# Three small reorderings in a decoder trunk: a split spread, conv taps inside the fourth slab, and two steps of the opening taken earlier

## The reference, cut to what matters

```
e = silu(c @ cond_w + cond_b)
shift, scale, gate = split(e @ ada_w[i] + ada_b[i])      # 9 vectors of 1024 for a layer
h = rms_norm(x, g) * (1 + scale) + shift
x = x + 0.5 * gate * ((silu(h @ w1) * (h @ w3)) @ w2)     # SwiGLU sublayers
u = glu(h @ w_in + b_in); v = depthwise_conv31(u) + dw_b  # Conformer
x = x + gate * (silu(layer_norm(v)) @ w_out + b_out)
```

## Time and profile before

| what | us |
|---|---|
| median of 3 runs | 1976.34 (1975.79 to 1976.45) |
| the profiled execution's own time | 1978.21 |
| its span in the trace | 1976.4 |
| TensorE matmuls busy | 1945.8 (98%) |
| VectorE busy | 1110.3 (56%) |
| ScalarE busy | 661.9 (33%) |
| GpSimd busy | 150.5 (8%) |
| DMA | 275.88 MB, mean 140 GB/s |

### The profile page before, as it was taken

One profiled execution on the slowest core, in us unless ns is written; L12 is line 12 of the kernel. 1 busy time (PEld: TensorE's weight loads), 2 busy tenths in 40 slices (PEclk: granted clock), 3 DMA queues, 4 the chain that ended last, 5 costly groups with the idle time before them and its releaser, 6 DMA issues.

```text
span 1976.4 us, 24087 instructions
## 1 busy us (share of the span) xinstructions
PE 1945.8 (98%) x9444; PEld 1562.6 (79%) x9444; DVE 1110.3 (56%) x1351; ACT 661.9 (33%) x742; POOL 150.5 (8%) x101
## 2 busy tenths in 40 slices
PE   6999999999989999999999999999999999999999
PEld 5788888876577888888888888888778788888887
DVE  4865564589888565633666533246569774333222
ACT  3422222242254322222432222234248743222211
POOL 0100000121411000001100000111022020000000
PEclk9999999999989999999999999999999999999999
DMA  9454544436413545432354522323245323222232
GB/s 394 170 206 176 206 165 166 158 106 180 126 55 138 208 174 194 175 124 93 116 213 170 191 93 79 102 100 124 95 99 137 107 86 107 85 106 85 88 98 90
DMA packets 50777, 275.88 MB, mean 140 GB/s; under 512 B 7456, under 2 KB 8096, under 8 KB 25760
## 3 DMA queue, kind: packets, MB, share of 16 engines
q1 hardware_dynamic: 47648, 270.87, 39.0%
q10 hardware_dynamic: 3072, 4.23, 0.9%
HBM read 251.94 MB, written 2.10 MB: 129 GB/s over the span
## 4 chain that ended last, share of the span: by engine, by line
PE 89%; DVE 4%; ACT 2%; issue 1%; DMA 0%; ACTq 0%; DVEq 0%; SPq 0%
PE ps L1491 27%; PE ps L1493 26%; PE ps L1492 26%; PE ps L1734 2%; PE ps L1512 1%; PE ps L1837 1%; PE ps L1853 1%; PE ps L1823 1%; PE ps L1619 1%; PE ps L1519 1%; DVE w L896 0%; PE ps L1532 0%; PE ps L1537 0%; PE ps L1531 0%; ACT h_hi L676 0%
## 5 line engine op out<-in xcount | busy, mean ns | idle before, releaser
L1491 PE MATMUL ps<-h_hi,w 128*128 128x512 f32 x1552 | 610.5, 393 | 1.2 <-DVE h_lo L995 1.0
L1493 PE MATMUL ps<-h_hi,w 128*128 128x512 f32 x1552 | 605.0, 390 | 0.0
L1492 PE MATMUL ps<-h_lo,w 128*128 128x512 f32 x1552 | 604.8, 390 | 0.0
L1491 PEld LDWEIGHTS ps<-h_hi,w 128*128 128x128 f32 x1552 | 291.7, 188 | 74.2 <-issue 12.8
L1493 PEld LDWEIGHTS ps<-h_hi,w 128*128 128x128 f32 x1552 | 291.5, 188 | 61.2
L1492 PEld LDWEIGHTS ps<-h_lo,w 128*128 128x128 f32 x1552 | 291.8, 188 | 58.8
L896 DVE TENSOR_TENSOR w<-raw,w 128x1408 fp32r<-128x1408 f32 (+1 forms) x104 | 201.0, 1933 | 204.4 <-ACT w L630 204.4
L630 ACT ACTIVATE w<-raw 128x1408 fp32r<-128x1408 f32 (+1 forms) x104 | 164.7, 1583 | 418.0 <-PE ps L1493 405.8
L1491 PE MATMUL ps<-g_hi,w 128*128 128x512 f32 x704 | 274.5, 390 | 0.0
L1493 PE MATMUL ps<-g_hi,w 128*128 128x512 f32 x704 | 274.2, 389 | 0.0
L1492 PE MATMUL ps<-g_lo,w 128*128 128x512 f32 x704 | 274.2, 389 | 0.0
(11 more groups left out here) (217 smaller groups left out, 1710.8 us busy)
## 6 DMA issues: line engine op xcount, KB each, us to landing
raw<-up_d SPq DMA_DIRECT2D x88, 1024.0 KB, 6.4
ada_raw<-ada_d SPq DMA_DIRECT2D x64, 1024.0 KB, 4.8
raw<-down_d SPq DMA_DIRECT2D x64, 704.0 KB, 4.1
raw<-mix_d SPq DMA_DIRECT2D x28, 1024.0 KB, 4.8
stage<-ada_d SPq DMA_DIRECT2D x12, 1024.0 KB, 20.1
stk<-parted SPq DMA_DIRECT2D x32, 256.0 KB, 4.0
stk<-parted SPq DMA_DIRECT2D x32, 128.0 KB, 2.3
u_blk<-u SPq DMA_DIRECT2D x48, 64.5 KB, 2.0
```

The source lines that it names most:

```text
L1491: pe.matmul(dst, a_hi_, b_hi_, start=start, stop=False, skip_group_check=True)
L1492: pe.matmul(dst, a_hi_, b_lo_, start=False, stop=False, skip_group_check=True)
L1493: return pe.matmul(dst, a_lo_, b_hi_, start=False, stop=stop, skip_group_check=True)
```

## The change

There are three edits.

1. Opening. On ScalarE `hi(N_UP[0] + 1)`, the rounding of slab 1, moves from behind the last chunk's square to the head of chunk 4, behind the wait for the second half of x. On TensorE `start_group(3)` moves from step 3 of the first slab to step 2.
2. `spread` is cut in two parts. For the six norms but the first, the high diagonal's matmul stays ahead of step 5; the low diagonal's and `bias_sums` come 3 matmuls later, between the two output chunks of step 5. (Norm 2 runs both together, as before.)
3. Conv. `conv_taps(0)` no longer stands ahead of `conv_in(3)`, but inside it, ahead of its step 2.

```
@@ ScalarE, opening
             for c in range(4, KD):
                 act.wait_ge(x_in_s[1], 16)
+                if c == 4:
+                    hi(N_UP[0] + 1)
                 entry_high(0, c)
                 square(0, c, x[:, c, :], x_in_s[1], 16)
-            hi(N_UP[0] + 1)
             root(0)
@@ TensorE, first_slab
-                    if k == 3 and m == 0:
+                    if k == 2 and m == 0:
                         start_group(3)
                     if k == 5 and m:
-                        spread(m)
-                        bias_sums(m)
+                        spread_part(m, 0)
                     ...
                     for b in range(2):
                         last = triple(...)
+                        if k == 5 and b == 0 and m:
+                            spread_part(m, 1)
+                            bias_sums(m)
@@ TensorE
+            def spread_part(m, part):
+                pe.wait_ge(rdiag_done, 2 * m + part + 1)
+                last = pe.matmul(row, ones_r[:, :], (fac_hi, fac_lo)[part], start=(part == 0), stop=(part == 1),
+                                 skip_group_check=True)
+                if part:
+                    last.then_inc(row_done, 1)
@@ TensorE, conv_in
+                if c == LAG + 1:
+                    two_chunks(c % 2, pair[c % 2], None, lambda: conv_taps(0), 2).then_inc(slab_done, 1)
+                    return
@@ TensorE, the loop
             for c in range(KD):
                 conv_in(c)
-                if c >= LAG:
+                if c > LAG:
                     conv_taps(c - LAG)
```

More of the change, by code:

```diff
@@ L1606, in sums @@
                 add(sq_tmp[:, 1, :], False, True, stat_done)
+            def spread_part(m, part):
[4 more added lines that the diff above has]
+                    last.then_inc(row_done, 1)
             def spread(m):
[L1610 to L1613, removed]
+                for part in range(2):
+                    spread_part(m, part)
             def ada_reduce(q):
```

## The result

| | before | changed |
|---|---|---|
| median, us | 1976.24 (1975.79 to 1977.04, 6 runs) | 1984.87 (1983.97 to 1985.43, 6 runs) |
| ratio | | 1.0043, 95% interval 1.0033 to 1.0053 |
| profiled execution, its span | 1978.21, 1976.4 | 1985.26, 1983.5 |

Slower by 8.6 us, where I had forecast 6.2 and a range up to 1984.6. The direction was right, the size was too small and the time lies outside the range. Between the two profiled executions there are 7.1 us, and they are to be seen at three places: the opening, the conv's slab 3 and the split spreads.

What follows compares the result with a forecast made beforehand. TensorE, busy 98% of the span, was taken as the bound. Opening + 1.4, spread - 0.5, conv + 3.6 and its clock + 1.7 sum to + 6.2 us: 1976.34 becomes 1982.5 us, eight-in-ten range 1979.8 to 1984.6.

Steps and rivals of the forecast that it cites:

- The conv's wait: Ahead of conv slab 3: TensorE idle 4.3 us in place of 0.8, waiting for VectorE's low half; + 3.6 us.
- The conv's clock: Behind the gap ahead of conv slab 3: granted clock falls to half speed; + 1.7 us.
- The spread: Five norms with a first slab: splitting removes the wait for the low diagonal, partly taken back by GpSimd; - 0.5 us.
- The opening: First slab's steps: ScalarE stands for slab 1's transfer, delaying chunk 4 and TensorE, with a likely clock fall; + 1.4 us.
- I take + 1.4, nearer to the fall: Opening's low spread: chosen between + 0.5 us without a clock fall and + 1.9 us with one.
- the start of step 4 at 39.2: Opening: TensorE starts step 4 at 39.2 in place of 37.51, after a gap of 2.7 us.
- The base: Whole kernel: the + 6.2 us sum from the 1978.21 us profiled execution, applied to the 1976.34 us median, giving 1982.5 us.
- The clock holds: Rival, opening and conv gaps: no clock fall in either, + 3.6 us in all, 1980.0 us; chance 0.07.
- The row that I argued from: Attention stage: TensorE stood 2.06 us, then the clock fell for 3.4 us, losing 1.7 us of matmul time.
- Long slow stretches: Rival, opening and conv gaps: longer half-speed stretches in both, + 8.1 us in all, 1984.4 us; chance 0.10.
- Slab 3's low half does not hold TensorE: Rival, conv: taps inside slab 3 just remove the 0.80 us wait; + 0.1 us in all, 1976.4 us; chance 0.05.
- slab 1 lands early: Rival, opening: slab 1 on the chip by 34.4, not 35.7; with the case before - 3.6 us, 1972.7; chance 0.04.

Runs made afterwards that it cites:

- experiment 7: Only the taps moved inside slab 3, with 18 extra matmuls filling the gap ahead of slab 3's wait, against the kernel before: 1981.05 against 1976.52 us.
- experiments 10 and 11: Against before, conv unchanged: 10 has group 3 ahead of step 2, slab 1 rounded behind chunk 7's high half, 1974.94 us; 11 adds the split spread, 1974.85 us.
- experiment 2: Only the opening's edit (slab 1 rounded ahead of chunk 4, group 3 ahead of step 2) against the kernel before: 1978.85 against 1976.37 us.
- experiment 1: The kernel before, unchanged, profiled once more: median 1976.48 against 1976.37 us, span 1974.8 us.
- experiment 8: Only the taps moved inside slab 3, with slab 3's rounding and low half made earlier, against the kernel before: 1983.73 against 1976.52 us.

## Why the prediction was wrong

**The conv's wait: right.** Slab 3's start, its releaser and the length of the gap came as worked out. Nothing was taken back behind it.

**The conv's clock: right in kind and size.** 1.7 predicted, 1.6 by experiment 7.

**The conv against the median: short by 0.8** (5.3 against 6.1). The 0.8 us wait for `u_blk`, which the edit takes away, I booked as a steady 0.80 of gain. It is there in only some executions, and where it is missing there is less to win. Over the nine profiles with the conv unchanged it is 0.35 on average, so this is worth some 0.45. The rest, about 0.3, I can't place: from norm 1's to norm 3's high spread these nine take 186.7 to 188.9 us, 187.5 on average. The wait for `u_blk` makes part of that spread; most of the rest is the slow stretch behind the conv, 10.2 us in seven of them and 13.6 in experiments 10 and 11, where the way from chunk 1's taps to norm 3 takes 145.1 us in place of 143.6 to 143.9. The changed kernel and edit 3 alone take 193.1 and 193.3.

**The spread: right.** - 0.5 predicted, - 0.6 in the traces.

**The opening: the mis-sized term.** + 1.4 predicted, + 2.5 by edit 1 alone, + 2.4 between the profiles. The step that failed is "I take + 1.4, nearer to the fall", and the start of step 4 at 39.2 under it; the runs showed + 2.4 to + 2.5 in its place. Four things went into it. I had found + 1.9 for the case of a fall and then took less, although my own argument said that a gap longer than 2.06 us brings one. The gap is 4.46 and not 2.7 us: step 3 ended about 1.0 us sooner, at 35.47, since the clock had risen later in the profile that I read (8 matmuls in 3.78 us, against 2.77 in the changed kernel's) than in any other but one, and step 4 began 0.7 later, at 39.93. The 0.7 is slab 1's: ScalarE had it at 36.4, not 35.7. By issue and time to landing it came at 35.3 to 36.4 over all profiles, past 36.0 in three, so this part is chance. The last part is the profile that I counted from: in experiment 2, with slab 1 there at 35.49 and step 4 at 39.01, the low spread stands at 49.29, only 1.6 us behind the 47.71 of my rows, but 2.4 behind the 46.85 of experiment 1. The mechanism held; the size was read from an opening that was itself 0.9 us late.

**The base.** I carried a sum made on one execution of 1978.21 to a median of 1976.34 as if its 1.87 us would stay in both. Experiment 1 shows where most of the profile's excess was: 0.86 us in the late clock and 0.66 in the wait for `u_blk`, just where the change works. The changed kernel has no such slack to give back, since in the opening it waits for a transfer and in the conv for VectorE. So the difference of medians is 8.6 where that of the profiles is 7.1, and the range, built round the profile's rows, was too low. In single edits the sum missed 1.1 in the opening, 0.8 in the conv and 0.3 in the spread's median (- 0.2, where the traces show - 0.6).

**The rivals.** "The clock holds" falls: all five profiles of kernels with an open gap of 3.8 to 4.5 us show the fall, six gaps in all. The row that I argued from is less firm than I took it: a wait of 2.06 to 2.10 us stands at that place of the attention stage in all thirteen profiles, and behind it the clock fell in eleven, not in experiments 10 and 11. "Long slow stretches" is nearest in time (1984.4) and wrong in mechanism: in the changed kernel each stretch was about 3.4 us. "Slab 3's low half does not hold TensorE" was priced on one gate; experiment 8 found the second, so it could not have come to 1976.4. That slab 1 lands early falls by every trace (35.3 us at the soonest); this rival was also booked as faster with - 3.6 us, which is inside the 3.95 us that I had called no change.

What stays open: which of the small differences between executions, the clock's rise in the opening, `u_blk`, and the start of the slow stretch behind the conv, make up the last 0.5 us. No run here separates them.

## What to carry to other kernels

Before a step is moved ahead in an in-order queue, read from the trace when its input lands, not when its output is wanted: the rounding found its slab behind chunk 7's high half and not ahead of chunk 4 (no place between was run), and the taps could trade places with slab 3 only after VectorE's low half and its gating, which ran under the very taps that were moved. Price a gap twice, by its length beyond the wait that was there (here 4.3, less 0 to 0.8) and by the half speed behind it (here 1.6). And profile the kernel before twice: what differs between its own executions is what a single profile's sum can't be trusted for.

## What the runs showed of the hardware that was not expected

A gap of about 4 us in dense matmuls cost 1.3 to 1.6 us more in its wake, and 16 or 18 matmuls with no use of their results, issued into the gap, bought that back: the clock stayed at 1.00, and the steps that waited started no later (31.86 against 31.85 us, 39.00 against 39.01). The wait itself stays: both medians still lie above before's, by 4.5 and 1.5 us. The Trainium skill (TensorE: Matmul & The Clock Gate, "HAM oscillation — how this bites in real kernels") tells of the fall behind a wait; these traces agree with it. A wait of 2.1 us in the attention stage was enough in eleven of thirteen profiles, and not always; in experiment 10 the clock stayed at 1.00:

```profile
1478.69 0.50 PE L1835 MATMUL ps<-sp_hi,con 128*128 128x512 f32 x1 [2.10 <-DVE sp_hi L1440]
...
1480.00:1481.00 1.00, 1.00 (x8) 0.93 (x7) 0.93 (x3) 1.00 (x2) 0.00 (x0) 1.00 0.97 197
```

The same 8 matmuls of the opening took 2.11 to 3.78 us over the thirteen profiles, since the clock rose early or late, and in the kernels with an unchanged opening the low spread lay anywhere from 46.1 to 47.7.
